# The first four slabs of a fused decoder layer: own banks, the norm's matmul inside the third, weights cut between input tiles and squares, eight input loads

## The reference

```
u = rmsnorm(h, attn_norm_g) @ w_in          # 512 x 2048 @ 2048 x N_IN
u_rwkv, u_fox = split(u)
# rwkv: token shift, then low-rank branches
u = u + (token_shift(u) - u) * mu
r, k, v, xw, xa, xg = split(u_rwkv)
w_log = -softplus(-(w0 + tanh(xw) @ w2)) - 0.5
a     = sigmoid(a0 + xa @ a2)
g     = sigmoid(xg) @ g2
# fox: causal attention whose logits get c[query] - c[key],
c = cumsum(log_sigmoid(f_raw + fgate_b))    # the forget gate, 16 heads
```

## Time and profile before

| what | value |
|---|---|
| median of 3 runs | 2845.57 us |
| lowest and highest | 2842.83 and 2849.9 us |
| profiled execution, its own time | 2851.47 us |
| its span in the trace | 2849.8 us |
| TensorE busy | 2745.6 us, 96% |
| VectorE, ScalarE, GpSimd busy | 1139.2, 1007.6, 215.9 us |
| mean granted clock of TensorE | 0.984 of full |

### The profile page before, as it was taken

How to read it: one execution, slowest core, us unless ns; L and a number is a source line. 1 busy time by engine, 2 the same in 40 slices (tenths; PEclk the granted TensorE clock), 3 DMA queues, 4 the chain that set the end, 5 groups by cost and what they waited for, 6 DMA issues and landing times.

```text
span 2849.8 us, 41116 instructions
## 1 busy us (share of the span) xinstructions
PE 2745.6 (96%) x15562; PEld 2173.3 (76%) x15562; DVE 1139.2 (40%) x1669; ACT 1007.6 (35%) x1427; POOL 215.9 (8%) x344
## 2 busy tenths in 40 slices
PE   7999999999999889999999999999999999999998
PEld 5776666666667558888888888888888888888787
DVE  6642652553454333333333333333333333334544
ACT  5434533543443443343322333223332222234421
POOL 2000110110120011100000000000000000001300
PEclk9999999999999989999999999999999999999999
DMA  4221221222212232232233222232222322223232
GB/s 162 76 81 56 67 83 39 78 68 61 64 59 75 89 109 98 96 103 96 91 91 105 96 96 97 87 108 98 96 94 86 105 98 96 96 87 105 96 121 78
DMA packets 107733, 255.34 MB, mean 90 GB/s; under 512 B 35144, under 2 KB 37704, under 8 KB 107624
## 3 DMA queue, kind: packets, MB, share of 16 engines
q1 hardware_dynamic: 106352, 249.73, 27.3%
q0 software_dynamic: 1280, 4.20, 0.4%
HBM read 244.90 MB, written 8.98 MB: 89 GB/s over the span
## 4 chain that ended last, share of the span: by engine, by line
issue 75%; PE 15%; POOL 3%; DVE 3%; ACT 2%; DMA 1%; SPq 1%; POOLq 0%; DVEq 0%; ACTq 0%
PE bank L291 4%; PE bank L288 4%; PE bank L292 4%; PE bank L325 2%; POOL probs L988 1%; POOL scratch_pool L116 1%; DMA x_raw<-xT 1%; DVE acc_x L1548 0%; DVE w_lo L283 0%; POOL sg_t L980 0%; ACT w_hi L276 0%; POOL acc_e L1763 0%; POOL carried L1015 0%; PE bank L447 0%; POOL M_t L1002 0%
## 5 line engine op out<-in xcount | busy, mean ns | idle before, releaser
L283 DVE TENSOR_TENSOR w_lo<-raw,w_hi 128x1024 fp32r<-128x1024 f32 (+1 forms) x476 | 542.0, 1141 | 973.9 <-ACT w_hi L276 963.9
L276 ACT ACTIVATE w_hi<-raw 128x1024 fp32r<-128x1024 f32 (+1 forms) x476 | 468.6, 987 | 1039.8 <-PE bank L292 994.6
L288 PE MATMUL bank<-hn_hi,w_hi 128*128 128x512 f32 x1664 | 648.1, 389 | 0.0
L292 PE MATMUL bank<-hn_hi,w_lo 128*128 128x512 f32 x1664 | 647.3, 389 | 0.0
L291 PE MATMUL bank<-hn_lo,w_hi 128*128 128x512 f32 x1664 | 647.3, 389 | 0.0
L288 PE MATMUL bank<-in_hi,w_hi 128*128 128x512 f32 x1086 | 472.4, 435 | 52.3 <-DVE in_lo L1536 11.6
L291 PE MATMUL bank<-in_lo,w_hi 128*128 128x512 f32 x1086 | 444.9, 410 | 0.0
L292 PE MATMUL bank<-in_hi,w_lo 128*128 128x512 f32 x1086 | 431.6, 397 | 0.0
L288 PEld LDWEIGHTS bank<-hn_hi,w_hi 128*128 128x128 f32 x1664 | 312.3, 188 | 65.6 <-issue 0.5
L292 PEld LDWEIGHTS bank<-hn_hi,w_lo 128*128 128x128 f32 x1664 | 312.3, 188 | 64.9
L291 PEld LDWEIGHTS bank<-hn_lo,w_hi 128*128 128x128 f32 x1664 | 312.3, 188 | 64.9 <-issue 0.5
(11 more groups left out here) (237 smaller groups left out, 2118.6 us busy)
## 6 DMA issues: line engine op xcount, KB each, us to landing
raw<-w_gu SPq DMA_DIRECT2D x176, 512.0 KB, 3.4
raw<-w_mix SPq DMA_DIRECT2D x136, 512.0 KB, 3.6
raw<-w_down SPq DMA_DIRECT2D x64, 384.0 KB, 3.1
raw<-w_down SPq DMA_DIRECT2D x64, 320.0 KB, 2.8
raw<-ple_gate SPq DMA_DIRECT2D x32, 512.0 KB, 3.5
x_raw<-xT SPq DMA_DIRECT2D x4, 1024.0 KB, 12.0
h_t<-xT SPq DMA_DIRECT2D x4, 1024.0 KB, 8.8
out<-h_t POOLq DMA_DIRECT2D x16, 256.0 KB, 2.3
```

Source lines behind the costliest of these rows:

```text
L276: nc.scalar.activation(w_hi[:, ring_slots(par2, half), 0:cols[half]], raw[:, half, 0:cols[half]], ACT.Copy).then_inc(hi_ready, 1)
L283: nc.vector.tensor_tensor(w_lo[:, s, 0:cols[half]], raw[:, half, 0:cols[half]], w_hi[:, s, 0:cols[half]].bitcast(F32), ALU.subtract).then_ ...
L288: nc.tensor.matmul(out, w_h, x_hi, start=start, stop=False, skip_group_check=True)
L292: return nc.tensor.matmul(out, w_l, x_hi, start=False, stop=stop, skip_group_check=True)
```

## The change

- The input comes in eight loads of two tiles (512 KB) where it came in four of four tiles. Slab 0's second half is still issued behind the first four tiles.
- On ScalarE and VectorE slab 0's second half is cut ahead of tile 6 and no longer ahead of tile 4; slab 1's first half ahead of tile 12 and no longer after tile 15. Slab 2's halves are cut between the squares and the sums.
- On ScalarE both halves of slab 3 are rounded before `rstd`, slab 4 is rounded after the first `act_arrival_lora`. On VectorE slab 3 is cut right after the sums, then slab 0 is evacuated, slab 4 cut, and slabs 1 and 2 evacuated.
- Slabs 0 to 3 go to four banks, `psum[0]`, `psum[1]`, `b3` and `b4`, and TensorE no longer waits for `tile_evacuated` in them. Slab 4 still waits for three evacuations.
- The norm's two matmuls stand in the middle of slab 2 (at kt = 8) and no longer behind slab 1.
- The later wait for the residual's load of the input is set to the renamed semaphore's count.

```diff
-    def multiply_slab(pe, n, par2, x_hi, x_lo, kts=(HALF, HALF), side=None, input_ready=None):
-        after(pe, tile_evacuated, n - 1)
+    def multiply_slab(pe, n, par2, x_hi, x_lo, kts=(HALF, HALF), side=None, bank=None, input_ready=None):
+        if bank is None:
+            after(pe, tile_evacuated, n - 1)
+            bank = psum[par2]
...
-    bank_b = [b3, b4, b5, b6, b7]
+    lora_bank = [*psum[0:2], b3, b4]
...
-    def evacuate(dve, n, par2):
+    def evacuate(dve, n, bank):
...
-        evacuate(dve, m, m % 2).then_inc(tile_evacuated, 1)
+        evacuate(dve, m, lora_bank[m]).then_inc(tile_evacuated, 1)
...
-            for i in range(4):
-                if i < 2:
-                    sp.dma_start(raw[:, i, :], d["w_mix"][0][:, i * HALF * P:(i + 1) * HALF * P]
-                                 ).then_inc(raw_landed[i], 16)
-                sp.dma_start(x_raw[:, 4 * i:4 * i + 4, :], x_quarter(i)).then_inc(S(f"input_landed_{i}"), 16)
+            for i in range(KT // 2):
+                if i in (0, 2):
+                    half = i // 2
+                    sp.dma_start(raw[:, half, :], d["w_mix"][0][:, half * HALF * P:(half + 1) * HALF * P]
+                                 ).then_inc(raw_landed[half], 16)
+                sp.dma_start(x_raw[:, 2 * i:2 * i + 2, :], d["xT"][2 * i:2 * i + 2].rearrange("k p t -> p k t")
+                             ).then_inc(S(f"x_landed_{i}"), 16)
...
 @block.tensor
-                multiply_slab(pe, n, n % 2, in_hi, in_lo,
+                def side(kt):
+                    if n == 2 and kt == HALF:
+                        pe.wait_ge(S("consts_landed"), 32)
+                        pe.wait_ge(S("ones_landed"), 32)
+                        pe.wait_ge(S("x_summed_dve"), KT // 2)
+                        pe.wait_ge(S("x_summed_pool"), KT // 2)
+                        for i in range(2):
+                            last = nc.tensor.matmul(aux[:], ones[:], acc_x[:, i, :], start=i == 0, stop=i == 1,
+                                                    skip_group_check=True)
+                        last.then_inc(S("norm_summed"), 1)
+                multiply_slab(pe, n, n % 2, in_hi, in_lo, side=side, bank=lora_bank[n],
                               input_ready=(lambda kt: pe.wait_ge(S("in_ready"), kt + 1)) if n == 0 else None)
-                if n == 1:
...
...
 @block.scalar
-                if kt % 4 == 0 and kt < 8:
-                    round_slab(act, 0, 0, halves=(kt // 4,))
-                act.wait_ge(S(f"input_landed_{kt // 4}"), 16)
+                if kt in (0, 6):
+                    round_slab(act, 0, 0, halves=(kt // 6,))
+                if kt == 12:
+                    round_slab(act, 1, 1, halves=(0,))
+                act.wait_ge(S(f"x_landed_{kt // 2}"), 16)
...
-            round_slab(act, 1, 1)
+            round_slab(act, 1, 1, halves=(1,))
             for kt in range(KT):
+                if kt in (8, 12):
+                    round_slab(act, 2, 0, halves=(kt // 12,))
...
-            for n in range(1, LORA_SLABS):
-                round_slab(act, n + 1, (n + 1) % 2)
-                if n == 1:
-                    rstd(rstd_x, NORM_X)
-                act_arrival_lora(act, n - 1)
+            round_slab(act, 3, 1)
+            rstd(rstd_x, NORM_X)
+            act_arrival_lora(act, 0)
+            round_slab(act, 4, 0)
+            act_arrival_lora(act, 1)
+            act_arrival_lora(act, 2)
...
 @block.vector
-                if kt % 4 == 0 and kt < 8:
-                    subtract_slab(dve, 0, 0, halves=(kt // 4,))
+                if kt in (0, 6):
+                    subtract_slab(dve, 0, 0, halves=(kt // 6,))
+                if kt == 12:
+                    subtract_slab(dve, 1, 1, halves=(0,))
...
-            subtract_slab(dve, 1, 1)
+            subtract_slab(dve, 1, 1, halves=(1,))
...
             for i in range(KT // 2):
+                if i in (4, 6):
+                    subtract_slab(dve, 2, 0, halves=(i // 6,))
                 dve.wait_ge(S("x_squared_even"), i + 1)
...
+            subtract_slab(dve, 3, 1)
...
+            dve_arrival_lora(dve, 0)
+            subtract_slab(dve, 4, 0)
+            dve_arrival_lora(dve, 1)
+            dve_arrival_lora(dve, 2)
             dve.wait_ge(S("aug_ones_ready"), 2)
             dve.wait_ge(S("u_column_cleared"), 1)
-            for n in range(1, LORA_SLABS):
-                subtract_slab(dve, n + 1, (n + 1) % 2)
-                dve_arrival_lora(dve, n - 1)
```

More of the change, by code:

```diff
@@ L305, in multiply_slab @@
                     input_ready(kt)
-                last = three_products(psum[par2][:], ring_slots(par2, half), k * P, x_hi[:, kt, :], x_lo[:, kt, :],
+                last = three_products(bank[:], ring_slots(par2, half), k * P, x_hi[:, kt, :], x_lo[:, kt, :],
                                       kt == 0, kt == sum(kts) - 1, burst)
@@ L733, in act_recurrence @@
                                  ).then_inc(S("Y_ready"), 1)
-    def evacuate(dve, n, par2):
+    def evacuate(dve, n, bank):
         dve.wait_ge(weights_used, 2 * n + 2)
-        return nc.vector.tensor_tensor(u_t[:, 1:SEQ + 1], psum[par2][:], rstd_x[:], ALU.mult)
+        return nc.vector.tensor_tensor(u_t[:, 1:SEQ + 1], bank[:], rstd_x[:], ALU.mult)
     def dve_arrival_rwkv(dve, s, g):
@@ L752, in dve_arrival_rwkv @@
             dve.wait_ge(S("fox_v_turned"), 2 * g)
-        evacuate(dve, n, (s - 1) % 2).then_inc(tile_evacuated, 1)
+        evacuate(dve, n, psum[(s - 1) % 2]).then_inc(tile_evacuated, 1)
         if kind == 1:
@@ L1276, in _ @@
             for n in range(LORA_SLABS):
-                multiply_slab(pe, n, n % 2, in_hi, in_lo,
-                              input_ready=(lambda kt: pe.wait_ge(S("in_ready"), kt + 1)) if n == 0 else None)
-                if n == 1:
[L1280 to L1287, removed]
+                def side(kt):
[9 more added lines that the diff above has]
+                multiply_slab(pe, n, n % 2, in_hi, in_lo, side=side, bank=lora_bank[n],
+                              input_ready=(lambda kt: pe.wait_ge(S("in_ready"), kt + 1)) if n == 0 else None)
             def group(g, gp):
@@ L1613, in out_pair @@
                     ffn_norm[1](dve, o, o)
-            dve.wait_ge(S("input_landed_0"), 32)
+            dve.wait_ge(S("input_landed_0"), 16)
             out_pair(0, False)
             for i in range(1, 4):
-                dve.wait_ge(S(f"input_landed_{i}"), 32)
+                dve.wait_ge(S(f"input_landed_{i}"), 16)
             with dve.Fori(1, OUT_SLABS // 2 - 1) as i:
```

## The result

The changed kernel takes 2854.63 us, the median of 7 runs (2850.09 to 2862.17), and the kernel before 2848.49 us in 7 runs (2840.43 to 2852.28). The ratio is 1.003, with a 95% interval from 1.0016 to 1.0044, which is 4.6 to 12.5 us. By the medians it is 6.1 us more and by the means 8.6; 6.9 were forecast. Single executions of one kernel lie up to 12 us apart, so the total is read from all of them, and what happened from the first 110 us of the traces, where most steps repeat to some tenths of a microsecond. A fall of the clock or a late landing moves them by 1 to 2 us, and the text says where.

The account below looks back on a forecast made before the run. TensorE, busy 96% of the span, was taken as the bound, with slab 4's start set by other engines' order. 4.8 us later start plus 2.1 slow clock gave +6.9: 2845.57 to 2852.5 us, range 2846 to 2858.

Parts of the forecast that it names:

- T4: Moment TensorE starts slab 4, used to price the whole change; forecast 74.8 against 70.02 us before.
- parts 3 and 4: Own banks end slab 3 near 61; the chain from the sums to slab 4 takes 32.8, starting it 4.8 us later.
- The cover of some 8 us: Time slab 4's load wait was hidden before, result at 55.06 with TensorE busy until 70.02; the change removes it.
- part 1: Input loads and ScalarE's order at the start: adds begin 1.5 us later, at 27.3; TensorE's 2.6 us stall costs nothing further.
- part 2: Slab 2's two subtractions inside VectorE's adds: sums end at 42.0 us, bounds 40.1 and 44.9, against 38.85 before.
- The sum of 42.8: End of the sums if no subtraction is absorbed under the shared port's exclusive lock, 0.8 us more than the 42.0 taken.
- part 5: After the long wait slab 4 begins at 1.2 GHz and loses ten slow steps: 2.1 us, bounds 0 and 2.1.
- z − T4: Time from slab 4's start to the z matmul inside it; the slow clock was to add 2.1 us.
- No binding order: Rival, chance 0.10: SP's and VectorE's order does not bind; early load gives slab 4 at 66.4, 2844.1 us, or 2836.5.
- Worth nothing: Rival, chance 0.12: the start's change moves T4 by less than 2 us; +2.2, 2847.8 us.
- Slower: Rival, chance 0.20: clock also falls in the wait before the bonus matmul, 1.6 us more; +8.5, or +9.3, 2854.9 us.

Follow-up runs that it names:

- c stored later: Changed kernel with SP's wait for the forget gate's result and its two stores moved behind the loads of slabs 4 and 5; slab 4 at 69.73 against 75.20 us.
- evacuations first: Changed kernel with slabs 1 and 2 evacuated before slab 4 is cut; slab 4 started at 70.67 against 75.20 us.
- slab 3 early: Changed kernel with slab 3's load issued before SP waits for the sums of squares; slab 4 started at 70.25 against 75.20 us.
- the root first: Changed kernel with the reciprocal root ahead of both roundings of slab 3 on ScalarE; slab 4 started at 74.67 against 75.20 us.
- all cures: Changed kernel, slab 1's half after tile 15, slab 3 loaded, slab 4 cut, slabs 1-2 evacuated earlier, c stored later: 0.9977 of kernel before; slab 5 cut earlier too: 0.9964.
- start alone: Kernel before with only the eight input loads and new rounding and cutting order at the start; slab 4 started at 71.16 against 70.02 us.
- two cures: Changed kernel with slab 3 loaded before the wait for the sums and c stored behind slabs 4 and 5's loads; 2841.6 us, ratio 0.9982 to the kernel before.
- TensorE kept busy: Changed kernel with 62 extra matmuls, results unread, between slabs 3 and 4; slab 4 at 75.57 against 75.20, z matmul at 81.03 against 82.81 us.

## Why the prediction was right

**What T4 waits for (parts 3 and 4).** Right, link by link. Forecast and measured: sums end 42.0 and 42.16; slab 3's load 43.4 and 43.58; root 53.5 and 53.33; forget gate 63.2 and 63.28; slab 4's load 64.1 and 64.16; slab 4 74.8 and 75.20. The cover of some 8 us that the prediction said would go did go. Inside the chain two landings missed and nearly cancelled: slab 3's second half was usable 1.2 us behind the first and not 1.65, and slab 4's first half 4.2 us behind its issue and not 3.5. Taking single links out moved slab 4 by 5.5 us (c stored later), 4.5 (evacuations first), 5.0 (slab 3 early), 1.1 (slab 1's half after tile 15) and only 0.5 (the root first, where 2.95 were forecast).

**The input's part (part 1).** TensorE started at 9.57 and not at about 10.2, the half landed at 20.0 and not 20.6, the adds began at 26.65 and not 27.3. That TensorE's start would not matter was right in both kernels; that tile 12's wait "costs nothing further" holds only where the norm's matmul is hidden. Where slab 3 was loaded early it was not, and the clock's fall at tile 12 then showed.

**The sums (part 2).** 42.16 against 42.0, but by luck in part. From the first add to the end it took 15.5 us; the prediction's terms give 15.4 (13.0 + 2.4), of which it took off 0.8 for subtractions that would be absorbed. In all, nothing was absorbed. The adds only began 0.65 earlier than forecast, and that made up for it. The first subtraction took 2.32 us beside GpSimd's add, the second 1.22, and the adds together 12.3 us (6.24 + 2.57 + 3.48) where they had taken 13.0. The Trainium skill (SBUF — State Buffer, "SBUF: two separate sides") has VectorE with two SBUF inputs wait as long as GpSimd holds the shared port; the 2.32 against 1.22 fits that. The sum of 42.8 that I drew from it was 0.6 too much because of the start of the adds alone; its length was right.

**The clock (part 5).** z − T4 grew from 5.44 to 7.61, 2.2 where 2.1 were said. The clock at 1.2 GHz was there, and with a warm clock z − T4 was 5.46. The 2.1 was one trace's number, though: in the variants with 8 to 15 us of idle time before slab 4, z − T4 lay between 7.48 (the root first) and 8.44 (c stored later), which is 2.0 to 3.0 us. And what the clock costs at z is not what it costs further on: with a warm clock the bonus matmul gains only 0.6, since the scan then waits for slab 5's cut. There the size of the term held, but its cause is shared.

**The sum.** +6.9 forecast, +6.1 by the medians and +8.6 by the means, +7.35 seen at the bonus matmul. The spans of the two profiled executions differ by only 1.9 us. The 7.35 us are still there at the second z matmul (9.0) and shrink behind it, and the clock goes with it: between 110 and 480 us the mean granted clock was 0.99 in the changed kernel's execution and 0.97 in that of the kernel before. That clock differs from one execution to the next, so this pair says nothing about the total.

**The rivals.** "No binding order" fell, and so did its arithmetic: it said slab 4 at 66.4 if the load alone came early, but VectorE is held by the forget gate (until 64.0 in that run), so the halves were cut only at 66.4 and slab 4 started at 69.73. "Worth nothing" fell at T4 = 75.20. "Slower", by a fall of the clock at the first bonus wait, did come in the profiled execution: 1.92 us for that matmul against 1.12, a clock of 0.50 from 107 to 110, and a second z matmul 9.0 us late and not 7.35, so 1.6 as priced. The second such wait, at which it fell before, was spared, so that nothing was added. That was luck: in four variants (c stored later, evacuations first, slab 1's half after tile 15, slab 3 early) the clock was at 0.50 to 0.52 behind both waits. How often the changed kernel pays this, its one trace can't say, and the rival is not refuted in full.

## What to carry to other kernels

A wait that is removed from the busiest engine is worth only what the next release allows. Before pricing it, follow the release of its next unit of work back through every in-order stream, queues included: here three items stood ahead of it by order alone, and moving two of them turned +6 us into -6. The change was not wrong in itself: the same two moves in the kernel before changed nothing, and with all cures on top of it -9 was reached. Which part of it (own banks, late norm, early cuts of slab 2) the gain needs was not tested one by one. And where an edit puts a long idle time ahead of a burst, look at who else works during the burst before booking the slow clock as a loss.

## What the runs showed of the hardware

- The granted clock is no function of the wait alone. Eight traces have the wait at tile 12. After 2.43, 2.41, 2.38, 2.37 and 2.17 us it stayed at 2.4 GHz (changed kernel, start alone, c stored later, evacuations first, two cures); after 2.42, 2.42 and 2.38 it fell to 1.2 (root first, slab 3 early, TensorE kept busy). After 1.95 us before slab 4 it fell too.
- A table load is hidden only where it is placed ahead of the wait: in the kernel with slab 3 early it ran before the wait for the norm's matmul, in the one with the root first behind it, 1.28 us on the chain. The switch cost 1.30 us from its start to the next activation (49.40 to 50.70 in the changed kernel), no more.
- Two halves of 512 KB issued 0.45 us apart were usable 1.2 to 1.9 us apart, and the difference went straight into the chain. The first of slab 3's halves landed 3.5 us after its issue in the changed kernel and 4.5 us after it with c stored later, at the same place in SP's order.
